# Two of the four weight sums of a mixed tile, made by loads and adding DMAs instead of VectorE

## The reference

```python
def swiglu(h, w_gate, w_up, w_down):
    return (jax.nn.silu(h @ w_gate) * (h @ w_up)) @ w_down
...
for i in range(DEPTH):
    h = h + 0.5 * swiglu(rms_norm(h, norms[i, 0]), ffn_w_gate[i, 0], ...)
    h = h + mixer_i(rms_norm(h, norms[i, 1]))        # attention + S5, or DSA + differential
    h = h + 0.5 * swiglu(rms_norm(h, norms[i, 2]), ffn_w_gate[i, 1], ...)
    h = h + sigmoid(rms_norm(h, norms[i, 3]) @ ple_w_gate[i]) * (p[i] @ ple_w_proj[i])
```

## Time and profile before

| | |
|---|---|
| median of 3 runs | 1891.37 us (1891.32 to 1891.4) |
| the profiled execution | 1889.01 us, its span 1887.2 us |
| TensorE busy | 1858.4 us, 98% of the span, at a granted clock of 0.998 |
| VectorE busy | 1354.8 us, 72% |
| ScalarE busy | 895.7 us, 47% |
| GpSimd busy | 260.9 us, 14% |
| DMA | 179.88 MB, mean 95 GB/s |

### The profile page before, as it was taken

The page is one execution under the profiler, slowest core; times in us unless marked ns, Lnnn a source line. Parts: engine busy times, 40 slices in busy tenths (PEclk is TensorE's granted clock), DMA queues, the critical chain, the costliest instruction groups (busy, mean ns, idle before and its releaser), DMA issues.

```text
span 1887.2 us, 31448 instructions
## 1 busy us (share of the span) xinstructions
PE 1858.4 (98%) x11418; PEld 1615.1 (86%) x11418; DVE 1354.8 (72%) x1983; ACT 895.7 (47%) x1509; POOL 260.9 (14%) x204
## 2 busy tenths in 40 slices
PE   8999999999999999999999999999989999999998
PEld 6899988777799998887899998877658899998886
DVE  8788788774988874357888864269984988874355
ACT  7455542245555563234455553244563655554222
POOL 0000001312100000234000001073243100000225
PEclk9999999999999999999999999999999999999999
DMA  5233333332233333323333332232101233333321
GB/s 180 90 112 101 99 106 105 96 100 86 78 98 95 109 112 111 111 67 101 100 92 99 111 123 96 93 109 68 57 1 46 91 100 99 111 105 118 105 74 56
DMA packets 56753, 179.88 MB, mean 95 GB/s; under 512 B 12144, under 2 KB 12144, under 8 KB 56656
## 3 DMA queue, kind: packets, MB, share of 16 engines
q1 hardware_dynamic: 54656, 173.69, 29.7%
q0 software_dynamic: 928, 3.02, 0.5%
q10 hardware_dynamic: 1088, 2.10, 0.3%
HBM read 175.04 MB, written 3.15 MB: 94 GB/s over the span
## 4 chain that ended last, share of the span: by engine, by line
PE 87%; DVE 9%; ACT 2%; POOL 1%; issue 1%; DMA 0%; DVEq 0%; SPq 0%; POOLq 0%; ACTq 0%
PE ps L2314 36%; PE ps L2276 26%; PE ps L2258 17%; PE ps L2762 2%; PE ps L2425 1%; DVE work L1256 1%; DVE sm L1280 1%; DVE stat L1254 1%; POOL sumsq L1556 1%; DVE x_lo L441 1%; ACT prob L1998 0%; PE ps L2476 0%; PE ps L2288 0%; DVE sm L1299 0%; PE ps L2711 0%
## 5 line engine op out<-in xcount | busy, mean ns | idle before, releaser
L389 DVE TENSOR_TENSOR w_lo<-raw,w_hi 128x1024 fp32r<-128x1024 f32 x174 | 231.6, 1340 | 217.0 <-ACT w_hi L381 216.3
L381 ACT ACTIVATE w_hi<-raw 128x1024 fp32r<-128x1024 f32 x186 | 194.2, 1054 | 293.9 <-PE ps L2276 248.7
L2314 PE MATMUL ps<-xs_hi,w_hi 128*128 128x256 f32 x1088 | 308.2, 283 | 0.5
L2314 PE MATMUL ps<-xs_lo,w_hi 128*128 128x256 f32 x1088 | 307.9, 283 | 0.0
L2314 PE MATMUL ps<-xs_hi,w_lo 128*128 128x256 f32 x1088 | 307.9, 283 | 0.0
L2276 PE MATMUL ps<-act_hi,w_hi 128*128 (+1 forms) x720 | 280.5, 390 | 0.0
L2276 PE MATMUL ps<-act_lo,w_hi 128*128 (+1 forms) x720 | 280.1, 389 | 0.0
L2276 PE MATMUL ps<-act_hi,w_lo 128*128 (+1 forms) x720 | 280.1, 389 | 0.0
L2258 PE MATMUL ps<-x_hi,w_hi 128*128 128x512 f32 x640 | 257.5, 402 | 8.5 <-ACT w_hi L381 7.2
L2258 PE MATMUL ps<-x_hi,w_lo 128*128 128x512 f32 x640 | 250.2, 391 | 0.0
L2258 PE MATMUL ps<-x_lo,w_hi 128*128 128x512 f32 x640 | 249.8, 390 | 0.0
(11 more groups left out here) (412 smaller groups left out, 3545.5 us busy)
## 6 DMA issues: line engine op xcount, KB each, us to landing
raw<-in_weights SPq DMA_DIRECT2D x322, 512.0 KB, 3.6
h<-in_xT ACTq DMA_DIRECT2D x4, 512.0 KB, 6.4
out<-result SPq DMA_DIRECT2D x4, 512.0 KB, 3.0
p_raw<-in_pT POOLq DMA_DIRECT2D x2, 512.0 KB, 4.2
scratch_u<-u_sc SPq DMA_DIRECT2D x1, 512.0 KB, 6.6
u_grp<-scratch_u SPq DMA_DIRECT2D x1, 512.0 KB, 4.1
scratch_y<-y_grp SPq DMA_DIRECT2D x2, 256.0 KB, 3.1
y_ch<-scratch_y SPq DMA_DIRECT2D x1, 512.0 KB, 3.6
```

The source lines that it names most:

```text
L381: act.activation(w_hi[:, slot], raw[:, slot], ACT.Copy).then_inc(hi_ready, 1)
L389: dve.tensor_tensor(w_lo[:, slot], raw[:, slot], w_hi[:, slot].bitcast(F32), SUB)\
L2314: last = pe.matmul(ps[:, bank, 0:HALF], w[:, at, cols], x[:, k], start=(start and k == 0 and part == 0), stop=(stop and k == KH - 1 and pa ...
```

## The change

The first addition of `weight_sums` goes. In its place ScalarE's queue issues two loads of 256 KB for each mixed tile (g0 and u1, straight from the weights in HBM into the two rows), and when both have landed, GpSimd's queue issues two DMAs of 256 KB that add u0 to each row (`accum_op=ADD`). Even tiles use `w_sum[0:2]`, odd tiles a new buffer `other_sums` over the start of `act_hi`. For the first two mixed tiles of an FFN the loads stand in the passage; from then on tile b+3's stand in tile b, after `own_hi(b+1, 1)` and ahead of `silu_right`, behind a wait for tile b+1's `t_ready` (its sums have been read) and `w_sums`. VectorE now waits for the adds ahead of its two remaining additions. ScalarE's loop is one turn shorter, and that turn is written out behind it, since the last tiles load nothing ahead. The chunks are still loaded into `raw` as before, so g0 and u1 are now read twice from HBM and u0 three times.

```diff
@@ weight_sums (VectorE)
-                dve.tensor_tensor(w_sum[:, 0:2], own[:, 0:4:3],
-                                  own[:, 2].unsqueeze(1).to_broadcast([P, 2, T]), ADD)\
+                dve.wait_ge(added(b), turns_of(f, i, b))
+                dve.tensor_tensor(w_sum[:, 2], loaded_sums(b)[:, 0], own[:, 3], ADD)\
                    .then_inc(fast["w_sums"], 1)
-                dve.wait_ge(fast["w_sums"], counted(3, f, i, b, 1))
-                dve.tensor_tensor(w_sum[:, 2], w_sum[:, 0], own[:, 3], ADD)\
-                   .then_inc(fast["w_sums"], 1)
-                dve.wait_ge(fast["w_sums"], counted(3, f, i, b, 2))
+                dve.wait_ge(fast["w_sums"], counted(2, f, i, b, 1))
                 dve.tensor_tensor(w_sum[:, 3], w_sum[:, 2], own[:, 1], ADD)\
                    .then_inc(fast["w_sums"], 1)
@@ fast_tile (VectorE)
+                dve.wait_ge(fast["t_ready"], counted(2, f, i, b, 2))
                 weight_sums(i, b + 1)
@@ GpSimd, once for each FFN
+        def block_sums(pool, f, first):
+            plain = PLAINS[f]
+            pair = plain // 2
+            def sums(i, b):
+                dst = loaded_sums(b)
+                up = A["weights"][bass.ds(i * 4 + (first + 2 * b + 1), 1)]\
+                    .rearrange("a p b f -> (a p) (b f)")
+                pool.wait_ge(loaded(b), turns_of(f, i, b))
+                pool.dma_start(dst[:, 0], up[:, 0:T], accum_op=ADD).then_inc(added(b), 16)
+                pool.dma_start(dst[:, 1], up[:, 0:T], accum_op=ADD).then_inc(added(b), 16)
...
+            with pool.Fori(pair + 1, NF // 2, 1) as i:
+                sums(i, 0)
+                sums(i, 1)
@@ ScalarE
+            def load_blocks(i, b):
+                gate, up = (A["weights"][bass.ds(i * 4 + (first + 2 * b + k), 1)]
+                            .rearrange("a p b f -> (a p) (b f)") for k in range(2))
+                dst = loaded_sums(b)
+                act.dma_start(dst[:, 0], gate[:, 0:T]).then_inc(loaded(b), 16)
+                act.dma_start(dst[:, 1], up[:, T:]).then_inc(loaded(b), 16)
+
+            def load_ahead(i, b):
+                act.wait_ge(fast["t_ready"], counted(2, f, i, b - 2, 2))
+                act.wait_ge(fast["w_sums"], counted(2, f, i, b - 2, 1))
+                load_blocks(i, b)
@@ opening_tile (ScalarE)
+                load_ahead(pair, 2)
                 copy_part(pair, 0, 0)
...
                 own_hi(pair, 1, 1)
+                load_ahead(pair, 3)
                 silu_right(pair, 0)
@@ fast_tile (ScalarE)
                 own_hi(i, b + 1, 1)
+                if ahead:
+                    load_ahead(i, b + 3)
                 silu_right(i, b)
@@ passages of six and of four (ScalarE), behind the last gained(...)
+                load_blocks(pair, 0)
+                load_blocks(pair, 1)
                 silu(0)
```

More of the change, by code:

```diff
@@ L276, in encoder @@
         w_sum = over("w_sum", [P, 4, T], at_square)
+        other_sums = over("other_sums", [P, 2, T], at_hi)
         act_f = over("act_f", [P, NF * T], at_lo)
@@ L408, in banks_of, with loaded, added, turns_of @@
             return ((5, 6, 7), (0, 1, 2))[b % 2]
+        def loaded(b):
+            return fast[("even_loaded", "odd_loaded")[b % 2]]
+        def added(b):
+            return fast[("even_added", "odd_added")[b % 2]]
+        def turns_of(f, i, b):
+            return i * 32 + (b // 2 + 1 + (FAST_BEFORE[f] - PLAINS[f]) // 2) * 32
+        def loaded_sums(b):
+            return other_sums[:] if b % 2 else w_sum[:, 0:2]
         def quarter(a, o):
@@ L517, in sums_lo @@
                 at = halves_of(first, b)[("T24", "T13")[which]]
-                src = w_sum[:, 2:4] if which == 0 else w_sum[:, 0:2]
+                src = w_sum[:, 2:4] if which == 0 else loaded_sums(b)
                 turned = isinstance(i, int) and 2 * i + b < plain + 2
@@ L1558, in sum_squares @@
                 pool.wait_ge(sum_step, done)
+        def block_sums(pool, f, first):
[8 more added lines that the diff above has]
+                pool.dma_start(dst[:, 1], up[:, 0:T], accum_op=ADD).then_inc(added(b), 16)
+            sums(pair, 0)
+            sums(pair, 1)
+            with pool.Fori(pair + 1, NF // 2, 1) as i:
+                sums(i, 0)
+                sums(i, 1)
         def s5_loads(pool):
@@ L1652, in _ @@
             sum_squares(pool, 4)
+            block_sums(pool, 2, STARTS[5])
             sum_squares(pool, 5)
@@ L1749, in sums_hi @@
                     act.wait_ge(fast["product"], counted(5, f, i, b - 1, (3, 5)[which]))
-                act.wait_ge(fast["w_sums"], counted(3, f, i, b, (3, 1)[which]))
+                if which == 0:
+                    act.wait_ge(fast["w_sums"], counted(2, f, i, b, 2))
+                else:
+                    act.wait_ge(added(b), turns_of(f, i, b))
                 act.activation(wf_hi[:, at], src, ACT.Copy).then_inc(fast["t_hi"], 1)
@@ L1794, in opening_tile, with fast_tile @@
                 own_hi(pair, 1, 1)
+                load_ahead(pair, 3)
                 silu_right(pair, 0)
-            def fast_tile(i, b):
+            def fast_tile(i, b, ahead=True):
                 copy_part(i, b, 0)
@@ L1897, in ffn_up_act @@
             fast_tile(pair, 1)
-            with act.Fori(pair + 1, NF // 2 - 1, 1) as i:
+            with act.Fori(pair + 1, NF // 2 - 2, 1) as i:
                 fast_tile(i, 0)
                 fast_tile(i, 1)
-            fast_tile(NF // 2 - 1, 0)
+            fast_tile(NF // 2 - 2, 0)
+            fast_tile(NF // 2 - 2, 1, ahead=False)
+            fast_tile(NF // 2 - 1, 0, ahead=False)
             last_tile(NF // 2 - 1, 1)
```

5 lines of the change are left out of this document (added).

## The result

The changed kernel takes 1967.26 us in the median (1963.58 to 1972.9, 4 runs), the kernel before beside it 1891.38. The ratio is 1.0404, 95% interval 1.0379 to 1.0429: 4% slower, where no change was forecast, and far outside the range. The profiled execution is the slowest of the four; its span of 1971.2 us is 84.0 more than before, where the medians differ by 75.9. Measured on TensorE's matmuls, the mixed tiles of the four FFNs last 181.60, 202.49, 178.71 and 204.73 us, where they lasted 161.60, 181.94, 161.60 and 181.95. So 80.4 of the 84.0 us are there.

A forecast was written before the change was run, and what follows sets the result against it. TensorE's matmuls alone were taken to bound the mixed tiles. Terms -0.3 + 0 + 1.2 + 0 + 0 = +0.9 us on the median 1891.37 gave 1892.3 us, forecast as no change; range 1890.8 to 1898.0.

The forecast's parts named there:

- What bounds the kernel: Mixed tiles: TensorE's matmuls alone, 0.12 us apart; taking work off VectorE can give back no more than 1.6 us.
- part 1: Mixed tiles: the removed addition frees 82.8 us of VectorE, covered by TensorE's stream; worth -0.3 us, bounds 0 and -1.6.
- The two extra 0.18 us of FFNs 2 and 4: Second mixed tile there: `weight_sums` comes late; this loss was taken as VectorE's and given back, 2 x 0.18 us.
- part 3: End of the opening tile: uncovered issues stop the next tile's third product 0.30 us, +1.2 us for four FFNs (+0.4 to +2.0).
- Part 2: Middle tile: ScalarE's wait and two issues, 0.87 us, end before `copy_part` 0 can start, still waiting for TensorE; cost 0.
- the sum: All five parts together: -0.3 + 0 + 1.2 + 0 + 0 = +0.9 us.
- Part 4: Issues ahead of the opening tile's `copy_part` 0 and four in the passage: handled beside running instructions, cost 0.
- rival (a): ScalarE's issues stand in line with its work, at opening tiles and passages: +5.4 us, 1896.8 us; chance 0.14.
- Part 5: Load and adding-transfer chain in each mixed tile: about 10 us from `t_ready`, in time for the sums; cost 0.
- The limit of 13.5 us: Mixed tiles: the time after `t_ready` by which the added sums are wanted; a longer chain costs time.
- The bounds, 7.2 and 16.4: Lower and upper ends, in us, for the chain of loads and adding transfers from `t_ready` on.
- rival (b): Adds land late in mixed tiles: 2.9 us in each of 30 two-tile turns, +87 us, 1978 us; chance 0.10.

The follow-up runs named there:

- four-buffer kernel: The changed kernel with four pairs of sum buffers in place of two, loads issued once the sums four tiles before are done; 1893.07 us, ratio 1.0010.
- the one without adding: The changed kernel with GpSimd's two adding transfers made plain ones, so its sums are wrong; 1896.99 us against 1891.57, ratio 1.0030.
- traffic-only kernel: The kernel before, plus the changed kernel's loads, wait and adding transfers from each FFN's third mixed tile, into a region nothing reads; 1915.45 us, ratio 1.0127.
- the one with wait and issues alone: The traffic-only kernel without GpSimd's adding transfers: ScalarE waits for `t_ready` and issues two loads; 1911.98 us against 1891.76, ratio 1.0107.
- the first try with four buffers and the early copy: The four-buffer kernel with `copy_part` 0 ahead of `residual_hi(6)` and load issues moved behind the next tile's third `copy_part`; 1910.68 us, ratio 1.0107.

## Why the prediction was wrong

**What bounds the kernel, and part 1: right.** VectorE lost 75.6 us, of 83 forecast, and nothing came of it. The two extra 0.18 us of FFNs 2 and 4 did come back where the sums were in time: in the four-buffer kernel the third tile of both is 10.08 us, where it was 10.16, and the second has part 3's stop alone.

**Part 2: right, on its condition, and with less room than it says.** In the median the first issue took 0.34 us, the second 0.38, and it started 0.52 after the first. In the four-buffer kernel and in the one without adding, with the same wait and issues at each tile's end, every middle tile from the third on is 10.08 us. Here are ScalarE of the latter at the end of a tile in FFN 2, and VectorE's last remainder:

```profile
604.54 0.34 ACTq L1773 DMA_DIRECT2D w_sum<-in_weights  x1
605.07 0.37 ACTq L1774 DMA_DIRECT2D w_sum<-in_weights  x1
605.61 0.38 ACT L1821 ACTIVATE t<-ps 128x256 f32<-128x256 f32 x1 [1.80 <-issue]
606.06 0.38 ACT L1811 ACTIVATE part_sum<-ps 128x256 f32<-128x256 f32 x1
```

```profile
603.08 1.22 DVE L536 TENSOR_TENSOR w_lo<-w_sum,w_hi 128x1024 fp32r<-128x1024 f32 x1
```

`t_ready` is given at 604.30, the first issue starts 0.24 us on and `silu_right` 1.31 us on, where 0.87 was taken. `copy_part` 0 can follow 0.30 behind that, about when TensorE lets it start anyway, so the cover was just enough. The condition was in the text: `weight_sums` comes later by the hold but is 1.2 us shorter. The traffic-only kernel lacks it, and its third products stop for 20 us.

**Part 3: right.** In FFNs 3 and 4 the second mixed tile takes 10.41 and 10.40 us, +0.33 and +0.24 against before, where 0.30 was worked out. In FFNs 1 and 2 it takes 10.61 and 10.67, since the second issue took 0.67 and 0.72 us there in place of 0.46. The four together lose 1.6 us, between the 1.2 of the sum and its upper end of 2.0.

**Part 4: right, and rival (a) wrong.** The opening tile is 10.40 us in all four FFNs, as before. ScalarE's timeline ahead of it in the changed kernel shows why:

```profile
77.55 1.06 ACT L1836 ACTIVATE x_hi<-xn 128x1024 fp32r<-128x1024 f32 x1 [3.13 <-PE ps L2323]
77.73 0.33 ACTq L1773 DMA_DIRECT2D w_sum<-in_weights  x1
78.09 0.46 ACTq L1774 DMA_DIRECT2D w_sum<-in_weights  x1
78.52 0.61 ACT L1792 ACTIVATE w_hi<-raw 128x512 fp32r<-128x512 f32 x1
```

Both issues are handled while the copy of 77.55 runs until 78.61. The rule of the Trainium skill (Advanced Engine Details and Errata, Sequencer and Instruction Queues), which the prediction set beside this part, holds here for DMA issues too. It holds while an issue's own wait is met: in the traffic-only kernel the unmet wait kept `silu_right` behind it.

**Part 5: here it failed.** "I take about 10, near the plain ones" was the step. By its terms, from `t_ready`, with the row of FFN 2:

| term | taken | measured |
|---|---|---|
| to the second load's issue | 0.43 | 0.79 |
| load lands | 3.1 (or 6.4) | 6.36 |
| to GpSimd's second issue | 0.58 | 1.16 |
| adding transfer lands | 4.5 for a plain one (3.1 to 9.0) | 7.32 |
| sum | 8.6 or 11.9, taken as about 10 | 15.6 |

The limit of 13.5 us was right. In the changed kernel a small sum's start is followed by its `t_ready` 6.7 us later, and 20.16 - 6.7 = 13.5. The bounds, 7.2 and 16.4, held the chain as well. What was wrong is the choice between them, and with it the 0.10 for rival (b). That rival gave 1978 us by the mechanism and at the place that the profile shows, where 1967.26 was measured. With the median over the late tiles, 16.27 us from `t_ready`, its own formula gives (16.27 - 13.5) x 30 = 83 us, and the mixed tiles lost 80.4.

Two things spoke against the choice, and I passed over both. The short landing (3.1 us) was that of two stores to a scratch tensor in HBM (`scratch_y<-y_grp`), in a stage with little other traffic, and not that of a load. The other one, 6.4 us, came from the stretch with a DMA share of 0.84, and the prediction itself put this kernel's share at 0.7 to 0.85. The crowded row, though of 512 KB, was the nearest one for the load. And the adding transfer, which the prediction itself took to read its target too, was given the landing of a plain one. With 6.4 for the load and the middle of its own 3.1 and 9.0 for the add, the chain is 13.5 us, on the limit: a chance of a half, not of a tenth. The page of the Trainium skill cited there (DMA: Bandwidth & Descriptors, Anatomy of one DMA) gave an estimate of 2.6 us for 256 KB. The measurement disagrees, with 5.3 to 6.4 us in this traffic, and 3.2 us for a plain transfer of GpSimd's queue.

**The sum lacked a term.** Kernels in which GpSimd issues these transfers end later: from the end of the last output's issue to the end of the span it is 3.8 us in the kernel before and in the one with wait and issues alone, 5.4 in the changed and the four-buffer kernel, and 4.8 in the traffic-only one. That is +1.6 us outside the mixed tiles, and its cause stays open. Another 1.8 us of the 84.0 lie ahead of the first mixed tile, a stretch that differs by up to 2.2 us between these runs, whatever the kernel.

## What to carry to other kernels

A buffer that is refilled by two transfers in a row is a ring of its own: release, issue, landing, issue, landing, use, release. Compare its length with the time that the buffers' tiles take before anything else, with landings read from a stretch as crowded as this one will be. When it is too long, the stops appear at other engines and other instructions, and the third product's 21 us here belonged to no cause of their own: removing the apparent cause only moved them. More lead (buffers) cures it where faster transfers can't be had (so it was with four buffers here), and every first use after a change of stage has to be counted by itself.

## What the runs showed of the hardware

- **An adding transfer costs the engines about twice a plain one.** GpSimd's queue took 12.5% of 1971.2 us for it, and 6.6% of 1894.2 us for the same bytes without adding; without the 0.5% of the transfers that every kernel has there, a ratio of 2.05.
- **Landings stretch in this traffic, at no cost to the engines' work.** The 512 KB loads into `raw` in the middle of the mixed tiles land in 3.7 us (median) before and in 6.4 in the changed kernel. In the four-buffer kernel the 256 KB landings are 7.0 to 8.0 us at a share of 0.71 (560 to 700 us), and the matmuls' pace stays 0.12 us. The share alone doesn't set them: with the same transfers issued behind the third copy (the first try with four buffers and the early copy), the loads land in 4.7 to 5.2 us at 0.74.
- **A stop costs more than its own length.** In the mixed tiles the matmul behind each of the changed kernel's 95 stops, and of the traffic-only kernel's 50, came up to 0.1 us later than the even pace asks.
- **TensorE's clock fell after some long stops**, of which the kernel before has none in its mixed tiles. The changed kernel's windows at the end of FFN 1 (clock, DMA share and GB/s last):

```profile
240.00:244.00 4.00, 3.95 (x33) 3.75 (x32) 1.39 (x2) 0.53 (x2) 0.00 (x0) 1.00 0.43 163
244.00:248.00 4.00, 2.15 (x11) 2.15 (x12) 3.38 (x5) 3.57 (x6) 0.00 (x0) 0.78 0.00 0
248.00:252.00 4.00, 4.00 (x30) 4.00 (x28) 3.62 (x6) 1.89 (x5) 0.00 (x0) 0.79 0.78 216
252.00:256.00 4.00, 4.00 (x36) 4.00 (x35) 0.49 (x2) 1.78 (x3) 0.00 (x0) 1.00 0.12 48
```

  TensorE stopped for 1.90 us there and then ran for some microseconds at the lower level (1.2 GHz); 0.78 and 0.79 are means over windows that hold both levels. Three such stretches of 3.4 us lie in the changed kernel's mixed tiles. They follow three of its five stops of 1.9 to 2.0 us; behind the other two the clock stayed at 1.00.
- **Open:** with plain transfers in place of adding ones the span went on for 8.4 us after the end of the last output's issue, where the four-buffer kernel has 5.4 and the kernel before 3.8. No run tells why. The order, 8.4 for plain and 5.4 for adding transfers on GpSimd's queue, speaks against the adding as the reason.
